# Two layers of attention in a long fused kernel: the grouped norm's steps moved within the order of work

## What is computed

```python
q_g = _rope(_rms(gq.reshape(B, T, GQA_HEADS, GQA_DIM), g_gqa_q), rope_large)      # 8 heads of 64
k_g = _rope(_rms(gk.reshape(B, T, GQA_KV_HEADS, GQA_DIM), g_gqa_k), rope_large)   # 2 heads of 64
q_pe = _rope(q[..., MLA_NOPE:], rope_small)       # q = (_rms(q_a, g) @ w_mla_qb), 4 heads of 96
...
for (q, k, v), (qc, kc, vc), s in zip(lat, cxt, scales):      # mla, diff, gqa
    o_lat.append(_latent_attention(q, concat(k, kc), concat(v, vc), s))
```

## Time and profile before

| | |
|---|---|
| median of three runs | 2404.79 us |
| profiled execution | 2402.75 us |
| its span | 2401.0 us |
| TensorE, VectorE, ScalarE, GpSimd busy | 2178.2, 1722.4, 1137.9, 65.8 us |
| granted TensorE clock, mean | 0.964 |

### The profile page before, as it was taken

The page is one execution under the profiler, slowest core; times in us unless marked ns, Lnnn a source line. Parts: engine busy times, 40 slices in busy tenths (PEclk is TensorE's granted clock), DMA queues, the critical chain, the costliest instruction groups (busy, mean ns, idle before and its releaser), DMA issues.

```text
span 2401.0 us, 37699 instructions
## 1 busy us (share of the span) xinstructions
PE 2178.2 (91%) x14571; PEld 1948.0 (81%) x14571; DVE 1722.4 (72%) x3358; ACT 1137.9 (47%) x1928; POOL 65.8 (3%) x83
## 2 busy tenths in 40 slices
PE   3998889999999999988987989799999988897998
PEld 2987889999997777978975676699989978667997
DVE  5667669889987887778866566577876665765554
ACT  2543444555554444444444455444444445454444
POOL 1000000000000000000001000100000000000000
PEclk9999989999999999999988999999999999998999
DMA  7648646664457887787841120477777753204664
GB/s 279 196 138 272 201 148 196 208 221 135 147 178 262 264 267 258 233 271 235 265 139 48 54 71 18 159 233 249 245 240 254 251 193 116 66 1 148 186 185 131
DMA packets 140016, 441.95 MB, mean 184 GB/s; under 512 B 15672, under 2 KB 38496, under 8 KB 139328
## 3 DMA queue, kind: packets, MB, share of 16 engines
q1 hardware_dynamic: 109440, 396.93, 51.5%
q10 hardware_dynamic: 25776, 23.97, 2.9%
q0 software_dynamic: 4624, 18.64, 2.2%
HBM read 425.72 MB, written 13.76 MB: 183 GB/s over the span
## 4 chain that ended last, share of the span: by engine, by line
PE 51%; DVE 13%; issue 10%; DMA 8%; ACT 4%; POOL 0%; ACTq 0%; DVEq 0%; POOLq 0%; SPq 0%
PE bk L1812 49%; DVE SPL L1172 3%; DMA TMP<-kept 3%; PE bk L1818 3%; DMA RAW<-in_peer 2%; ACT SPL L809 1%; DMA kept<-TMP 1%; DVE R L1172 1%; DVE RAW L1206 1%; ACT R L811 1%; DVE ST L1187 1%; DVE R L1181 1%; DVE TMP L1172 1%; DMA HID<-kept 1%; DVE EXT L1206 1%
## 5 line engine op out<-in xcount | busy, mean ns | idle before, releaser
L1172 DVE TENSOR_TENSOR SPL<-RAW,SPL 128x1024 fp32r<-128x1024 f32 (+1 forms) x614 | 746.6, 1222 | 349.7 <-ACT SPL L809 348.7
L809 ACT ACTIVATE SPL<-RAW 128x1024 fp32r<-128x1024 f32 (+1 forms) x614 | 645.0, 1054 | 618.0 <-PE bk L1812 297.6
L1812 PE MATMUL bk<-HH,SPL 128*128 128x256 f32 x3840 | 747.5, 288 | 19.3 <-DVE SPL L1172 8.5
L1812 PEld LDWEIGHTS bk<-HH,SPL 128*128 128x128 f32 x3840 | 621.2, 194 | 26.8 <-issue 11.4
L1812 PE MATMUL bk<-SPL,WHL 128*128 128x512 f32 x2328 | 553.5, 392 | 14.1 <-DVE WHL L1172 9.0
L1812 PE MATMUL bk<-HL,SPL 128*128 128x256 f32 x1920 | 547.2, 285 | 0.0
L1812 PEld LDWEIGHTS bk<-SPL,WHL 128*128 128x128 f32 x2328 | 428.5, 188 | 107.1 <-issue 21.4
L1812 PEld LDWEIGHTS bk<-HL,SPL 128*128 128x128 f32 x1920 | 372.7, 194 | 2.5
L1812 PE MATMUL bk<-SPL,HH 128*128 128x256 f32 (+1 forms) x1664 | 315.8, 292 | 32.7 <-DVE SPL L1172 17.5
L1812 PEld LDWEIGHTS bk<-SPL,HH 128*128 128x128 f32 x1664 | 269.0, 199 | 41.5 <-issue 26.8
L809 ACT ACTIVATE R<-bk 128x256 f32<-128x256 f32 (+4 forms) x350 | 168.9, 498 | 217.1 <-PE bk L1812 192.4
(11 more groups left out here) (139 smaller groups left out, 1974.9 us busy)
## 6 DMA issues: line engine op xcount, KB each, us to landing
RAW<-in_peer SPq DMA_DIRECT2D x256, 512.0 KB, 4.7
RAW<-in_ada SPq DMA_DIRECT2D x144, 512.0 KB, 4.9
RAW<-in_ffn SPq DMA_DIRECT2D x132, 512.0 KB, 4.4
RAW<-in_win SPq DMA_DIRECT2D x96, 512.0 KB, 4.5
RAW<-in_ffd SPq DMA_DIRECT2D x66, 512.0 KB, 4.3
RAW<-in_wout SPq DMA_DIRECT2D x32, 512.0 KB, 4.8
kept<-TMP ACTq DMA_DIRECT2D x88, 128.0 KB, 3.3
TMP<-kept ACTq DMA_DIRECT2D x66, 128.0 KB, 5.3
```

Of the source, the lines that this page charges most:

```text
L809: ins = e.activation(out, in_, func, bias=bias, scale=scale)
L1172: e.tensor_tensor(out, a, b, op).then_inc(*dve.up(*points))
L1812: ins = e.matmul(out, lhsT, rhs, start=start, stop=stop, skip_group_check=True)
```

## The change

For the latent in both layers: `gn_a` is placed right behind `pj 6` and its rows; `gn_b` ahead of `nm 13` and `qpe` instead of behind both; `gn_c` stands ahead of row 16 as before; `gn_d` moves from behind row 17 to ahead of row 18; and the four transposes kk and pg, woven before over rows 16 to 23 with `gn_c` and `gn_d`, are woven over rows 20 to 23.

```diff
     if s:
         ...
-    rest += [("pj", l, s, 0)] + keys + [("scl", l, s, "q"), ("pj", l, s, 6)] + turned + [("lr1", l, s, "q"), ("gn_a", l, s)]
-    rest += queries + [("gn_b", l, s)] + [("tr", l, s, "qa", i) for i in range(2)]
-    return first, rest, [("gn_c", l, s), ("gn_d", l, s)] + heads
+    rest += [("pj", l, s, 0)] + keys + [("scl", l, s, "q"), ("pj", l, s, 6), ("gn_a", l, s)] + turned + [("lr1", l, s, "q")]
+    rest += queries[:2] + [("gn_b", l, s), ("qpe", l, s)] + [("tr", l, s, "qa", i) for i in range(2)]
+    return first, rest, heads
+
+
+def narrow_rows(l, s, rows, heads):
+
+    a, b, c, d = [rows.index(("as", l, s, n)) for n in (16, 18, 20, 24)]
+    return [("gn_c", l, s)] + rows[a:b] + [("gn_d", l, s)] + rows[b:c] + weave(heads, rows[c:d])
 ...
-    plan += [("vt", 0)] + weave(others, rows[:mla]) + weave(heads, rows[mla:gqa]) + rows[gqa:-16] + [("sil2", 1)] + rows[-16:]
+    plan += [("vt", 0)] + weave(others, rows[:mla]) + narrow_rows(0, 0, rows, heads) + rows[gqa:-16] + [("sil2", 1)] + rows[-16:]
 ...
-    plan += [("vt", 1)] + weave(others, rows[:mla]) + weave(heads, rows[mla:gqa]) + rows[gqa:]
+    plan += [("vt", 1)] + weave(others, rows[:mla]) + narrow_rows(1, 0, rows, heads) + rows[gqa:]
```

## The result

The changed kernel has 2416.05 us, the median of 20 runs (2407.34 to 2422.42), against 2404.97 us for the kernel before, also the median of 20. The ratio is 1.0053, with a 95% interval of 1.0039 to 1.0066: the medians lie 11 us apart, and the interval says 9 to 16 us slower. The forecast was 2409.6 us in a range up to 2415.0. Its sign was right, and so were nearly all the waits that it read from the queues; its size was less than half of what came, because it had the cost of the slow clock wrong.

A forecast was written before the change was run, and what follows sets the result against it. TensorE was taken to bound the stage except in a few holes. Traded holes summed to +2.4 us per site, twice that +4.8 us, giving 2409.6 us on the median; range 2400 to 2415.

The forecast's parts named there:

- Step 1: gn_a ahead of maximum 14: TensorE's hole before lr2 q grows from 2.12 to 4.67 us, cost 2.55 us.
- Step 2: lr2 q, row 15, lr2 q (5.44 us): slow clock reaches half a microsecond further; maximum 15 comes 3.0 us later.
- Step 3: gn_b ahead of nm 13 and qpe: hole before the qa transposes 6.1 us, was 2.48; cost 3.6 us.
- Step 4: gn_d, kk and pg later: 4.85 of the 5.25 us kk hole gained, shared bank costs 1.0 us.
- The step that failed: Slow clock behind the hole before qa: the 1.4 us of rows 18 and 19 merely moves, bounds −1.4 and +1.5 us.
- The check by holes: TensorE's idle holes per site summed: 10.63 us before, 12.95 after, so +2.3 us.
- Rival D: Clearly slower: qa transposes become the bound, both groups at low clock; 5.4 us per site, 2415.6 us; chance 0.08.
- Rival B: The 5.25 us hole goes, its price hidden in VectorE's idle time; 2391.5 us, half of it about 2398; chance 0.13.

The follow-up runs named there:

- holes filled: Kernel before or after plus unread matmuls in TensorE's holes: before's order 0.9955, repeated 0.9988; after's order 0.9996, all against the kernel before.
- the rows' part alone: Kernel before with only gn_d ahead of row 18 and kk and pg over rows 20 to 23: ratio 0.9998, sites 37.38 and 37.14 us.

## Why the prediction was wrong

Four filled and unfilled sites divide the loss:

| | clock as granted | holes filled, clock 1.00 | cost of the clock |
|---|---|---|---|
| order of before | 36.22 us | 33.16 us | 3.06 us |
| order of after | 42.11 us | 36.73 us | 5.38 us |
| the change | +5.89 us | +3.57 us | +2.32 us |

So of the 5.9 us per site 3.6 us are the order of the queues and 2.3 us the clock. The forecast's site was 38.6 us (36.2 and 2.4), 1.9 above the 36.73 of its order at full clock: it held 1.9 us of slow clock where the run had 5.4. The difference is 3.5 us.

- **Step 1** held: 2.55 us forecast, the hole is 4.58 rather than 2.12 us, 2.46 more. gn_b had its power early and could not use it.
- **Step 2** was mis-sized. The group was to take about half a microsecond longer, at most 1.4; it took 2.32 longer (7.76 against 5.44). The bound of 1.4 came from eight shorter instructions, rows 18 and 19; at full clock this group takes 4.10 us, so that its half clock over the whole costs 3.66, of which the kernel before already paid 1.34. Part of that ran behind row 15 and went into the hole that follows; part ran ahead of it, so that maximum 15 came 3.4 us later and not 3.0. Against the forecast that is 0.5 us: the qa transposes came 7.17 us later, counted from row 14, against 6.7 by the forecast's own times (1435.70 to 1442.4).
- **Step 3** held: from maximum 15 to the qa transposes it takes 7.69 us (1436.41 to 1444.10) and 7.65 by the forecast; the hole is 4.87 and not 6.1 us because the group ended later.
- **Step 4** held for the queues: the kk hole is 0.39 us (0.4 forecast), the second kk transpose waits 0.78 (1.0 forecast). With the clock held up, row 16 to av 4 takes 17.89 us (1439.67 to 1457.56); the forecast's times give 17.8 (1444.7 to 1462.5).
- **The step that failed** is the last of the sum, the slow clock after the hole before qa: "I take it as the same sum moved". It was not in the sum. The 4.3 us by which step 4 makes the way from row 16 to av 4 shorter were counted against a stretch that held the slow rows 18 and 19, and the way after was worked out at full clock; the slow work was credited where it left and charged nowhere. In the run it came back bigger: 1.2 us from the qa transposes to row 16 (3.45 against 2.27) and 1.8 to 1.9 from there to av 4 (19.69 us, against 17.8 forecast). Together with 0.5 us before qa that is 3.5 us per site, the whole of the miss.
- **The check by holes** agreed with the sum (12.95 against 10.63) and was no check: it counts idle time, and slow work is not idle. Holes grew by only 1.4 us, the site by 5.9.
- **Rival D** described what happened: both groups at the low clock, 5.4 us per site, 2415.6 us, and it decides "once both holes are followed by 0.50 over their whole groups", which is what the stretch from 1431 to 1452 shows. It had a chance of 0.08; the range ended 1 us short of the result. That its total came so near is in part luck: it put 1.5 us on the group and 1.5 on rows 16 and 17, where against the forecast they cost 0.5 and, with the qa transposes, 3.0; and the hole before these did not pass 6 us.
- **Rival B** fell at the point given against it: maximum 15 stands ahead of gn_b and VectorE sat idle for 6.78 us in front of it.

The rule cited in step 2 (the Trainium skill, "TensorE: Matmul & The Clock Gate", Part 1: throttled by default, released by activity) spoke against the change and was right. The runs agree in both directions: with the change's longer holes the half clock lasted longer, and with the holes filled there was none. The sum needed the size as well, and here 7.76 us of work without a pause did not release the clock.

## What to carry to other kernels

An idle hole on TensorE has two prices, the wait and the speed of what comes after it; when a change moves or lengthens a hole, write the slow work down at its new place and cost the work there at half speed, and don't use the sum of idle time as a check. Before a step of a side chain is pulled ahead of the step that frees the bound engine, look for a blocking wait in that engine's queue between the chain's parts: here gn_b's early power was of no use behind maximum 15, and its 3.9 us delayed qpe. Where a hole on TensorE can't be closed, matmuls that nobody reads, sized to end before the hole does, hold the clock; here they were worth 3.1 us per site, and 5.4 in the changed order.

## What was not expected of the hardware

- Continuous work did not bring the clock back for a long time: the lr2 group ran for 7.76 us without a pause, all of it at half clock, after a hole of 4.6 us (kernel after, both layers); in layer 1 of the run with gn_a alone the same group got it back on the way (5.92 us).
- The same hole has two outcomes in one execution: 2.12 us before lr2 q was followed by a 4.07 us group in layer 0 and a 5.46 us one in layer 1 (kernel after with gn_a back), and there the sites differ by 1.8 us. With gn_b alone it was the other way round, 5.45 and 4.07 us, and the sites were alike. A kernel with such holes can carry that scatter between its runs.
- The length of a hole does not tell by itself. In the kernel before the 2.12 us hole was followed by the half clock and the 2.48 us one, 5.44 us of work later, was not (granted 1.00 from 1435.70 to 1437.30, the transposes 1.49 us), in both layers alike. With the rows' part alone the work behind holes of 1.53 and 2.26 us, with 0.6 us of transposes between them, ran at half clock just as it did behind 5.25 us at a stretch; whether the first of the two had a part in it no run shows.
